# A conformer, expert and attention block on one core: the residual of the second half kept on rows

## The reference, cut to what matters

```python
def rmsnorm(x, g):
    xf = x.astype(jnp.float32)
    y = xf * lax.rsqrt(jnp.mean(xf * xf, axis=-1, keepdims=True) + EPS)
    return (y * g.astype(jnp.float32)).astype(x.dtype)

def swiglu(x, w_gate, w_up, w_down):
    return (jax.nn.silu(x @ w_gate) * (x @ w_up)) @ w_down

# first block ends:  x = x + hierarchical_moe(h, ...);  x = rms_norm(x, norm_final_g)
x = x + 0.5 * swiglu(rmsnorm(x, g_ffn1[l]), w1_gate[l], w1_up[l], w1_down[l])
h = rmsnorm(x, g_mix[l])
p = h @ w_in[l]
...
x = x + jnp.concatenate([out_a, out_b], axis=-1) @ w_out[l]
x = x + 0.5 * swiglu(rmsnorm(x, g_ffn2[l]), w2_gate[l], w2_up[l], w2_down[l])
return rmsnorm(x, g_final)
```

## Time and profile before

| what | value |
|---|---|
| median of 3 runs | 2198.71 us (2197.13 to 2199.1) |
| profiled execution, device time | 2198.78 us |
| its span, first to last instruction | 2196.8 us |
| mean granted TensorE clock | 0.957 of 2.4 GHz |
| busy share: PE, PEld, DVE, ACT, POOL | 91, 62, 46, 25, 10% |
| DMA | 352.8 MB, 161 GB/s over the span |

### The profile page before, as it was taken

How to read it: one execution, slowest core, us unless ns; L and a number is a source line. 1 busy time by engine, 2 the same in 40 slices (tenths; PEclk the granted TensorE clock), 3 DMA queues, 4 the chain that set the end, 5 groups by cost and what they waited for, 6 DMA issues and landing times.

```text
span 2196.8 us, 24780 instructions
## 1 busy us (share of the span) xinstructions
PE 2003.1 (91%) x8821; PEld 1372.9 (62%) x8822; DVE 1004.5 (46%) x1482; ACT 560.0 (25%) x836; POOL 226.3 (10%) x257
## 2 busy tenths in 40 slices
PE   7999999969888999875999999899888899999998
PEld 6888887843222333224788878776435577888785
DVE  5998954441111111115644432434996444444323
ACT  4235335320000000003222221321427532222212
POOL 2000000011111122113000000202313310000000
PEclk9999999979999999987999999999899899999998
DMA  6432222759999999944233322233000022333221
GB/s 195 139 96 87 87 96 77 275 209 401 419 419 419 419 406 381 420 199 143 78 99 99 97 88 98 82 86 98 20 0 1 1 77 87 97 98 98 89 97 46
DMA packets 146684, 352.84 MB, mean 161 GB/s; under 512 B 27726, under 2 KB 85379, under 8 KB 121402
## 3 DMA queue, kind: packets, MB, share of 16 engines
q1 hardware_dynamic: 140602, 343.54, 42.7%
q0 software_dynamic: 6000, 8.42, 1.1%
q10 hardware_dynamic: 16, 0.00, 0.0%
HBM read 347.44 MB, written 15.73 MB: 165 GB/s over the span
## 4 chain that ended last, share of the span: by engine, by line
PE 72%; DVE 10%; DMA 9%; ACT 4%; issue 2%; POOL 2%; SPq 1%; POOLq 0%; DVEq 0%; ACTq 0%
PE psum L449 17%; PE psum L451 17%; PE psum L450 17%; DMA arena<-in_w_expert_up_dram 9%; PE psum L1253 8%; PE psum L1261 4%; PE psum L1920 2%; DVE w_lo L444 1%; DVE arena L2201 1%; DVE stat_mean L2198 1%; POOL arena L406 1%; PE psum L1949 1%; ACT w_hi L439 1%; PE psum L1244 1%; PE psum L1936 1%
## 5 line engine op out<-in xcount | busy, mean ns | idle before, releaser
L444 DVE TENSOR_TENSOR w_lo<-w_raw,w_hi 128x1024 fp32r<-128x1024 f32 x232 | 291.3, 1257 | 616.7 <-ACT w_hi L439 616.7
L449 PE MATMUL psum<-h_hi,w_hi 128*128 128x512 f32 x1312 | 519.8, 396 | 50.6 <-DVE w_lo L444 18.3
L450 PE MATMUL psum<-h_lo,w_hi 128*128 128x512 f32 x1312 | 517.0, 394 | 0.0
L451 PE MATMUL psum<-h_hi,w_lo 128*128 128x512 f32 x1312 | 516.7, 394 | 0.0
L439 ACT ACTIVATE w_hi<-w_raw 128x1024 fp32r<-128x1024 f32 x232 | 245.8, 1060 | 915.3 <-PE psum L451 870.9
L449 PEld LDWEIGHTS psum<-h_hi,w_hi 128*128 128x128 f32 x1312 | 250.6, 191 | 109.1 <-issue 43.5
L450 PEld LDWEIGHTS psum<-h_lo,w_hi 128*128 128x128 f32 x1312 | 250.4, 191 | 52.4 <-issue 0.2
L451 PEld LDWEIGHTS psum<-h_hi,w_lo 128*128 128x128 f32 x1312 | 250.1, 191 | 52.5
L1253 PE MATMUL psum<-arena,w_raw 128*64 128x512 f32 x832 | 204.2, 637 | 34.3 <-DMA arena<-in_w_expert_up_dram 33.6
L947 DVE SCALAR_TENSOR_TENSOR arena<-arena,vec 128x512 f32<-128x512 f32 x240 | 162.4, 743 | 1.0 <-ACT arena L777 1.0
L1253 PEld LDWEIGHTS psum<-arena,w_raw 128*64 128x64 f32 x832 | 60.0, 145 | 156.8 <-issue 109.5
(11 more groups left out here) (306 smaller groups left out, 2149.6 us busy)
## 6 DMA issues: line engine op xcount, KB each, us to landing
arena<-in_w_expert_gate_dram SPq DMA_DIRECT2D x22, 2048.0 KB, 24.5
arena<-in_w_expert_up_dram SPq DMA_DIRECT2D x22, 2048.0 KB, 29.2
arena<-in_w_expert_down_dram SPq DMA_DIRECT2D x22, 2048.0 KB, 22.5
w_raw<-in_w_in_dram SPq DMA_DIRECT2D x44, 512.0 KB, 3.7
w_raw<-in_w_gate_dram SPq DMA_DIRECT2D x88, 256.0 KB, 2.8
w_raw<-in_w_up_dram SPq DMA_DIRECT2D x88, 256.0 KB, 3.0
w_raw<-in_w_down_dram SPq DMA_DIRECT2D x44, 512.0 KB, 3.5
expert_down_third<-in_w_expert_down_dram SPq DMA_DIRECT2D x10, 2048.0 KB, 22.7
```

The source lines that it names most:

```text
L444: eng.tensor_tensor(wlo[:, s, :, :], raw[:, slot, :, :], whi[:, s, :, :].bitcast(F32), ALU.subtract).then_inc(w_lo, 1)
L449: eng.matmul(o, w_h, x_h, start=first, stop=False)
L450: eng.matmul(o, w_h, x_l, start=False, stop=False)
L451: return eng.matmul(o, w_l, x_h, start=False, stop=last)
```

## The change

The residual of the second half stays on token rows (`rows_tok`, in the memory of `xT`). The down projections and the output projection exchange their operands (`mul_rows`), half of the width after the other, without loops. The residual is added tile by tile (`residual_rows`), squares are summed along rows on ScalarE, and the next stage's operands are turned on TensorE half by half (`turn_half`) and split straight from PSUM (`turned_high`, `turned_low`). The scale of each row is put on a diagonal and spread by one matmul with ones (`spread`). At the end rows are normed and stored with no transposes. The output projection's operands get buffers of their own. The gains of the two final norms are loaded as rows into `sq`. GpSimd's sums of squares are gone. The small tensors move ahead of the wide ones, so that `xT` and all wide buffers after it begin on a multiple of 512 bytes (before: 416 bytes past one).

```diff
+ROWS_G = (G_WO, G_DN[0], G_MO, G_DN[1])
+TURNED = (19, 32, 39)
...
+sb("up_to_a_boundary", 8)
...
+        ohi_ = c4.enter_context(nc.sbuf_tensor("attention_hi", [P, KT * T], F32R))
+        c4.enter_context(nc.sbuf_tensor("attention_gap", [P, 256], F32))
+        olo_ = c4.enter_context(nc.sbuf_tensor("attention_lo", [P, KT * T], F32R))
...
+def seen(g):
+    return g // 2 + 1 + sum(1 for g0 in TURNED if g0 <= g and g0 % 2 == g % 2)
...
+def rows_ready(eng, stage, half, t):
+    if t < TT - 1:
+        eng.wait_ge(x1_r, (TT - 1) * (2 * stage + half) + t + 1)
+    else:
+        group_read(eng, ROWS_G[stage] + half)
+def turn_half(eng, bt, half, ready=None):
+    for t in range(TT):
+        if ready is not None:
+            ready(t)
+        for k in range(4 * half, 4 * half + 4):
+            mm = eng.transpose(psum[:, bt + k % 4, t * P:(t + 1) * P], rows_tok[:, t, k * P:(k + 1) * P], ident)
+            if t == TT - 1:
+                mm.then_inc(rows_t, 1)
+def turned_high(eng, n, bt, gain, ks):
     for k in ks:
...
+        eng.wait_ge(rows_t, n * KT + k + 1)
+        eng.activation(hhi[:, k, :], psum[:, bt + k % 4, :], ACT.Identity, scale=gain[:, k:k + 1]).then_inc(hi_r, 1)
+def turned_low(eng, n, bt, gain, ks):
     for k in ks:
...
+        eng.wait_ge(hi_r, n * KT + k + 1)
+        eng.scalar_tensor_tensor(out=hlo[:, k, :], in0=psum[:, bt + k % 4, :], scalar=gain[:, k:k + 1],
                                  in1=hhi[:, k, :].bitcast(F32), op0=ALU.mult, op1=ALU.subtract).then_inc(lo_r, 1)
...
+def square_row(eng, out, src, total):
+    eng.wait_ge(rsq_r, cnt["rsq"])
+    eng.activation(out, src, ACT.Square, accum_out=total).then_inc(rsq_r, 1)
+    cnt["rsq"] += 1
+def square_half(eng, stage, half, ts):
+    for t in ts:
+        rows_ready(eng, stage, half, t)
+        square_row(eng, junk[:, :], rows_tok[:, t, half * HALF:half * HALF + HALF],
+                   stat(R_B if half else R_A, t))
+def mean_of_first(eng, squares_):
+    eng.wait_ge(rsq_r, squares_)
+    eng.tensor_scalar(stat(R_SUM), stat(R_A), 1.0 / D, EPS, ALU.mult, ALU.add).then_inc(mean_r, 1)
+def root_of_halves(eng, means):
+    eng.wait_ge(mean_r, means)
+    eng.wait_ge(rsq_r, cnt["rsq"])
+    for t in range(TT):
+        eng.activation(stat(X_SQ, t), stat(R_B, t), ACT.Sqrt, bias=stat(R_SUM, t), scale=1.0 / D).then_inc(rroot_r, 1)
+def on_diagonal(eng, scales, n):
+    eng.tensor_tensor(diag.rearrange("p (t q) -> p t q", q=P), ident.unsqueeze(1).to_broadcast([P, TT, P]),
+                      scales.unsqueeze(2).to_broadcast([P, TT, P]), ALU.mult).then_inc(diag_r, 1)
+def invert_roots(eng, roots_, n):
+    eng.wait_ge(rroot_r, roots_)
+    dlink(eng, eng.reciprocal(stat(X_INV), stat(X_SQ)))
+    on_diagonal(eng, stat(X_INV), n)
+def spread(eng, n, bt):
+    eng.wait_ge(diag_r, n)
+    eng.matmul(psum[:, bt, :], ones, diag, start=True, stop=True).then_inc(bc_r, 1)
+def spread_read(eng, n, bt):
+    eng.wait_ge(bc_r, n)
+    eng.tensor_copy(stat_std[:, :], psum[:, bt, :]).then_inc(evac[(bt // 4) % 2], 1)
+    eng.wait_ge(evac[(bt // 4) % 2], seen(TURNED[n - 1]) - 1)
+def first_group(eng, c0, g, n, ready, spread_at):
+    bt = 4 * ((g + 1) % 2)
+    group_read(eng, g - 2)
+    for k in range(4):
+        eng.wait_ge(lo_r, n * KT + max(2 if n == 4 else 4, 2 * k + 2))
+        mul_chunk(eng, c0, k, g, (2 * k, 2 * k + 1), hhi, hlo, k == 0, k == 3)
+        if k == 0:
+            ready()
+            turn_half(eng, bt, 1)
+        if k == spread_at:
+            spread(eng, n - 3, bt)
...
+def mul_rows(eng, c, g, kts, xh, xl, first, last):
+    s = c % SPLIT
+    eng.wait_ge(w_lo, c + 1)
+    tiles_ = [(a, t) for t in range(TT) for a in range(CK)] if last else [(a, t) for a in range(CK) for t in range(TT)]
     for a, t in tiles_:
         f = slice(t * P, t * P + P)
-        o, kt = bank(g, t), 2 * k + a
-        eng.matmul(o, xh[:, kt, f], whi[:, s, a, :], start=(kt == 0), stop=False)
+        o, kt, end = bank(g, t), kts[a], last and a == CK - 1
+        eng.matmul(o, xh[:, kt, f], whi[:, s, a, :], start=(first and a == 0), stop=False)
         eng.matmul(o, xl[:, kt, f], whi[:, s, a, :], start=False, stop=False)
-        mm = eng.matmul(o, xh[:, kt, f], wlo[:, s, a, :], start=False, stop=(kt == KT - 1))
-        if kt == KT - 1 and t < TT - 1:
+        mm = eng.matmul(o, xh[:, kt, f], wlo[:, s, a, :], start=False, stop=end)
+        if end and t < TT - 1:
             mm.then_inc(row_done, 1)
     mm.then_inc(w_used, 1)
...
+def residual_rows(dve, stage, half, used, scale=None, ts=range(TT)):
+    g = ROWS_G[stage] + half
+    for t in ts:
         if t < TT - 1:
-            dve.wait_ge(row_done, (TT - 1) * half + t + 1)
+            dve.wait_ge(row_done, (TT - 1) * (2 * stage + half) + t + 1)
         else:
-            dve.wait_ge(w_used, C_WO + 4 * half + 4)
-        rows = x1_tok[:, t, half * HALF:half * HALF + HALF]
-        ins = dve.tensor_tensor(rows, bank(G_WO + half, t), rows, ALU.add)
-        ins.then_inc(x1_r if t < TT - 1 else evac[(G_WO + half) % 2], 1)
+            dve.wait_ge(w_used, used)
+        rows = rows_tok[:, t, half * HALF:half * HALF + HALF]
+        if scale is None:
+            ins = dve.tensor_tensor(rows, bank(g, t), rows, ALU.add)
+        else:
+            ins = dve.scalar_tensor_tensor(out=rows, in0=bank(g, t), scalar=scale, in1=rows, op0=ALU.mult,
+                                           op1=ALU.add)
+        ins.then_inc(x1_r if t < TT - 1 else evac[g % 2], 1)
...
+    sp.dma_start(sq_[:, :], A["norm_final_g"].rearrange("(o d) -> o d", o=1).to_broadcast([P, D])).then_inc(tables_in, 16)
...
+def sum_rows(dve, t):
+    dve.wait_ge(y_in[t], 16)
+    dve.tensor_tensor(rows_tok[:, t, :], y_tok[:, t, 0, :], rows_tok[:, t, :], ALU.add).then_inc(moe["pair"], 1)
+    dve.wait_ge(moe["pair"], t + 1)
+    dve.tensor_tensor(rows_tok[:, t, :], y_tok[:, t, 1, :], rows_tok[:, t, :], ALU.add).then_inc(moe["sums"], 1)
...
+row_junk = ar3[:, 8192:9216]
...
+    if j == 0:
+        load_rows(sp, 0)
+        load_rows(sp, 1)
+        load_group(0, ks=(0,))
+        load_rows(sp, 2)
+        load_rows(sp, 3)
+        load_group(0, ks=(1, 2, 3))
+        load_group(1)
...
+    if j:
+        sp.dma_start(sq_[:, :], A["g_final_2"].rearrange("(o d) -> o d", o=1).to_broadcast([P, D])).then_inc(
+            tables_in, 16)
+    for n in range(2 * N_UP):
+        half, kp = n // N_UP, n % N_UP
+        load_chunk(sp, C_DN[j] + n, (C_DN[j] + n) % RAW,
+                   down[:, 2 * kp:2 * kp + 2, half * CN:half * CN + CN])
 def pe_ffn(pe, j):
...
     if j == 0:
...
+        turn_half(pe, 4, 0, lambda t: pe.wait_ge(moe["sums"], t + 1))
+        first_group(pe, C_UP[j], G_UP[j], 4, lambda: pe.wait_ge(lo_r, 4 * KT + 4), 3)
+    else:
+        first_group(pe, C_UP[j], G_UP[j], 6, lambda: group_read(pe, G_MO + 1), 2)
...
+    for half in range(2):
+        g = G_DN[j] + half
+        group_read(pe, g - 2)
+        for kp in range(N_UP):
+            pe.wait_ge(flo_r, N_UP * j + kp + 1)
+            mul_rows(pe, C_DN[j] + N_UP * half + kp, g, (2 * kp, 2 * kp + 1), ahi, alo, kp == 0, kp == N_UP - 1)
+            if j == 0 and half == 1 and kp == 1:
+                group_read(pe, g - 1)
+                turn_half(pe, 4, 0)
+def act_ffn(act, j):
...
+        for t in range(TT):
+            if t == TT - 1:
+                act.wait_ge(gain_r, 2)
+                turned_high(act, 4, 4, both_gains, range(4))
+            act.wait_ge(moe["sums"], t + 1)
+            square_row(act, row_junk, rows_tok[:, t, :], stat(X_SQ, t))
+        group(0, ks=(1,))
+        act.wait_ge(rsq_r, cnt["rsq"])
+        act.activation(stat(X_INV), stat(X_SQ), ACT.Sqrt, bias=eps_col, scale=1.0 / D).then_inc(rroot_r, 1)
+        group(0, ks=(2,))
+        turned_high(act, 4, 4, both_gains, range(4, KT))
+        for t in range(TT):
+            if t == 2:
+                group(0, ks=(3,))
+            act.wait_ge(x3_r, t + 1)
+            square_row(act, row_junk, rows_tok[:, t, :], stat(V_SQ, t))
+        act.wait_ge(rsq_r, cnt["rsq"])
+        act.activation(stat(V_INV), stat(V_SQ), ACT.Sqrt, bias=eps_col, scale=1.0 / D).then_inc(rroot_r, 1)
+    else:
+        square_half(act, 2, 1, range(TT - 1))
+        group(0, ks=(1,))
+        square_half(act, 2, 1, (TT - 1,))
+        root_of_halves(act, 5)
+        group(0, ks=(2,))
+        turned_high(act, 6, 4, gain_of("g_ffn2_2"), range(4, KT))
+        group(0, ks=(3,))
...
+    for n in range(SPLIT, 2 * N_UP):
+        split_hi(act, C_DN[j], n)
+        if n == N_UP + 1:
+            square_half(act, 1 + 2 * j, 0, range(TT))
+        if j == 0 and n == N_UP + 3:
+            turned_high(act, 5, 4, gain_of("g_mix_2"), range(4))
 def dve_ffn(dve, j):
...
+            if k == 1 and g == 1 and isinstance(i, int):
+                spread_read(dve, 1 + 2 * j, 4)
             split_lo(dve, C_UP[j] + 4 * g, k, i, step)
...
+    if j == 0:
+        sum_rows(dve, 0)
+        sum_rows(dve, 1)
```

(102 more changed lines are left out.)

306 lines of the change are left out of this document (48 added, 258 removed).

## The result

The changed kernel takes 2127.2 us (median of 4 runs, 2125.12 to 2127.87) against 2198.78 before (4 runs): ratio 0.9672, 95% interval 0.9657 to 0.9686, 71.6 us less. The forecast was 2136, its range 2114 to 2154. The profiled execution is the fastest of the four, 2125.12 us with a span of 2123.1.

What follows compares the result with a forecast made beforehand. TensorE, busy 2003 of 2196.8 us, was taken as the bound, with losses at four seams. Gains of 23.3 + 10.7 + 11.2 + 17.6 = 62.8 us against 2198.78 gave 2136 us; range 2114 to 2154.

Steps and rivals of the forecast that it cites:

- Four seams: Experts to first feed-forward, to mixer, mixer output to second feed-forward, and the end: together 62.8 us gained.
- a rival's small end: Expert weight loads one fiftieth faster from the new address: 5.5 us gained, time 2130.
- tolerances of the seams: Uncertainty allowed in the forecast: 4 us on the first seam either way, 3 us on each other.
- The exchange at nothing: Dense matmuls with activation stationary and weight moving: same 24 matmuls per chunk, 0.2267 us each, no cost.
- rival of slower code: Down projections as 22 chunks of straight code issue matmuls slower; 0.290 us each gives 2203; chance 0.03.
- First seam: Experts to first feed-forward: 33.1 us lost instead of 56.4, a gain of 23.3 including 1.8 at the down projection.
- Middle seams: Mixer and second feed-forward starts: 3.9 us lost at each instead of 14.6 and 15.1.
- the 1.8 us of the gated product: Start of each down projection: finishing half 0 first removes TensorE's wait, gaining 1.8 us in each of two.
- The room of 0.6 us: Start of the down projection: the third weight chunk's low part is ready 0.6 us before TensorE asks.
- The end: Last matmul to end of span: 8.8 us instead of 26.4, VectorE being the queue; gain 17.6.
- Addresses: Wide buffers moved to a multiple of 512 bytes: bounded between nothing and 68 us, taken as no gain.
- The rival that named them: The new address speeds the experts' weight loads, whose queues moved 419 GB/s: time 2130, chance 0.12.

Runs made afterwards that it cites:

- Experiment 2: The changed kernel with its wide buffers put back to 416 bytes past a multiple of 512: 2134.6 us, ratio 0.9703.
- experiment 8: Changed kernel, two versions: gain row loaded earlier, first weight chunk after all row loads, last tile stored in halves or its scaling divided among engines; 2124.7 and 2124.6 us.
- Experiment 4: The changed kernel with half 0 turned and split only after the projection's last matmul, at both middle seams: 2138.8 us, ratio 0.9721.
- experiment 5: The changed kernel with both down projections taking the two halves of the width in turn, as the kernel before did: 2137.9 us, ratio 0.9725.
- experiment 6: The changed kernel with ScalarE squaring all 1024 columns of each row tile at the end, none of half 0 ahead: 2127.8 us, ratio 0.9677.
- experiments 1: Kernel before, only wide buffers moved: on a multiple of 512 bytes 2192.4 us, 256 past 2191.8, 128 past 2199.4, 64 past 2199.0.
- experiment 3: The changed kernel run once more, unaltered, giving its second profile: 2127.7 us, ratio 0.9671.

## Why the prediction was right, and where it was off

- **Four seams as the whole of the gain from the rows:** right, and right by size. Experiment 2 takes the address away and leaves 2134.6, against a sum of 2136. The measured 2127.2 is 8.8 below the sum. It lies in the stated range because the range was stretched by a rival's small end and by the tolerances of the seams; the sum itself had no term for the difference.
- **The exchange at nothing:** right. The 528 matmuls of the second down projection start between 1995.48 and 2114.94, 0.2267 us apart, in straight code and on rows. The rival of slower code did not come about.
- **First seam:** the first dense chunk was forecast 27.5 us after the experts and came 26.8 after (27.0 in the second profile), group 1 54.9 and 53.9 (55.1). Two sizes were wrong, in opposite directions. The fourth sum was forecast 23.5 us after the experts and came 24.0 after, at 994.02. The step to it was right: the sum follows from when the row loads land. The first landed 2.3 us later after the experts than before, not 1.2 (experiment 8 gives the same 2.3 back when the gain row moves), and the last 3.0 later, not 2.5. It landed at 991.51, and its first add began 0.02 us after that, just as VectorE was done with the tile before:

```profile
990.34 1.22 DVE L1573 TENSOR_TENSOR xT<-arena,xT 128x1024 f32<-128x1024 f32 x1
991.53 1.23 DVE L1571 TENSOR_TENSOR xT<-arena,xT 128x1024 f32<-128x1024 f32 x1
992.79 1.23 DVE L1573 TENSOR_TENSOR xT<-arena,xT 128x1024 f32<-128x1024 f32 x1
```

  Two adds take as long as one load, so a faster last load alone would not have moved the sum. From the fourth sum to the first chunk it was 2.9 us where 4.0 were forecast. The clock was charged 2.5; the first chunk, 5.60 us from its first start to its last end at full speed, took 1.6 more in this profile and 2.7 in the next. The wait for the copy of the scales, 0.7 forecast, is 0.87.
- **Middle seams:** 4.3 in each instead of 3.9. Experiment 4 shows that the early turning carries about half of it, 5.2 us of the 10.3 and 10.8 gained at each; which part of the rest (the squares, the root, the short reciprocal) gives the other half was not tested. That half after half carries the 1.8 us of the gated product is shown by experiment 5, where it costs 2.0 and 2.1. The room of 0.6 us that was left for `w_lo` behind it held: no such wait stands in the changed kernel's projections after the experts.
- **The end:** 7.8 instead of 8.8, VectorE's queue in the main, as forecast (experiment 6). The last tile was ready 4.8 us after the last matmul, not 5.5, and the store took 3.0, not 3.3.
- **The failed step is "Addresses", "I take nothing".** It is 7.0 to 7.6 us, by experiments 1 and 2, and most of the 8.8 between 2136 and 2127.2. "No operation that this trace times differs by address" was true of a trace in which all wide buffers lay off the grain. The argument was that the experts' matmuls have the short pitch at odd addresses; this was sound for TensorE, whose 0.2267 us are the same at either address, and said nothing of the queues. The rival that named them was given 0.12 and the time 2130. Its row was in hand: a DMA share of 1.02 while TensorE stood, in seven windows. The Trainium skill (DMA: Bandwidth & Descriptors, How a descriptor splits into AXI transactions) states 256 bytes as the grain on which reads begin, and the trace agrees for the side that is written, 427 against 418 GB/s. An estimate by its count of beats has the loss shrink with the bytes before the start, from 5 of some 260 beats at 160 bytes to 2 at 64, and there the trace differs: 418 GB/s at 64 and 128 bytes past, 419 at 160.
- **How the rate turns into time.** TensorE's waits for loads, the kernel before and the same on 512:

```profile
PE psum L1253 <- DMA arena<-in_w_expert_up_dram: 33.6, 12, 4.3
...
PE psum L1253 <- DMA expert_input<-in_w_expert_up_dram: 11.1, 6, 3.6
```
```profile
PE psum L1254 <- DMA arena<-in_w_expert_up_dram: 32.5, 12, 3.5
...
PE psum L1254 <- DMA expert_input<-in_w_expert_up_dram: 9.7, 4, 3.4
```

44.7 and 42.2 us: 2.5 of the 5.5 us by which the stretch is shorter (509.1, 503.6). Over all profiles these waits are 44.2 to 46.8 us off the grain and 41.1 to 42.8 on it, 3.0 less in the mean, of the 6.3 by which the stretch differs. By the granted clock over the stretch (0.949 to 0.956 off the grain, 0.955 to 0.959 on it) TensorE is at the low level for 44.8 to 51.9 us off the grain and 41.3 to 45.1 on it, 5.2 less in the mean, which is worth at most 2.6: waits and clock together account for most of it. The small end of the rival, one fiftieth of the rate over seven windows, 5.5 us, was near the right size; its time of 2130 was right within 3 us.
- What two profiled executions of one kernel differ in (experiment 3), 2.5 us in all, comes with no edit; the medians carry the comparison.

## What to carry to other kernels

Where transfers bound a stage, look at the SBUF start of what they write: on a multiple of 256 bytes the queues moved 2% more here, at no cost but the order of the allocations. A seam between dense stages closes if the next stage's operands are made from the half of the output that is done early; the form on rows makes that possible, and by itself brought about half of the gain at the middle seams here. When pricing work hidden in a chunk of a double-buffered stream, count the slack of the second slot too (about 2.9 us here), and price a pause with the clock behind it: 5.2 us for 3.3 us of standing here.
